# A two-block transformer kernel: a new order of the first loads and turns, and of two short stretches of products

## The reference, cut to what matters

```python
hn = rms_norm(h, norm1_g[i])            # h = x, (256, 1024)
z = hn @ w_in[i]                        # (1024, 3208)
qa, ka, va, qb, kb, vb, ob, ib, fb, uc, vc = split_cols(z, IN_SPLITS)
ya = stick_breaking_attention(qa, ka, va)
qk = jax.nn.silu(causal_depthwise_conv(jnp.concatenate([qb, kb], axis=-1), conv_w[i], conv_b[i]))
hb = mlstm_chunkwise(qb, kb, vb, ib + igate_b[i], fb + fgate_b[i])
...
```

## Time and profile before

| | |
|---|---|
| median of 3 runs | 1088.3 us (1086.83, 1088.3, 1090.26) |
| the profiled execution, its own time | 1087.57 us |
| its span | 1085.6 us |
| PE busy | 1058.6 us, 98% |
| DVE, ACT, POOL busy | 866.3, 714.3, 144.1 us |
| moved from HBM | 230.85 MB, 214 GB/s over the span |

### The profile page before, as it was taken

The page is one execution under the profiler, slowest core; times in us unless marked ns, Lnnn a source line. Parts: engine busy times, 40 slices in busy tenths (PEclk is TensorE's granted clock), DMA queues, the critical chain, the costliest instruction groups (busy, mean ns, idle before and its releaser), DMA issues.

```text
span 1085.6 us, 17366 instructions
## 1 busy us (share of the span) xinstructions
PE 1058.6 (98%) x6390; PEld 925.0 (85%) x6390; DVE 866.3 (80%) x1142; ACT 714.3 (66%) x962; POOL 144.1 (13%) x96
## 2 busy tenths in 40 slices
PE   7999989999999999999999999999999999999997
PEld 6877778888788887789989899998788889999986
DVE  5498689999999999877666777677777877876876
ACT  6676479898889898775435545445566766455553
POOL 3001100000000000012000334250200000432420
PEclk9999999999999999999999999999999999999999
DMA  9541528889988888754654454554433335545531
GB/s 369 189 155 39 206 82 347 348 346 333 346 331 337 343 344 334 285 209 156 225 180 178 155 213 161 206 193 155 173 137 118 116 120 211 207 156 217 184 126 40
DMA packets 33605, 232.64 MB, mean 214 GB/s; under 512 B 3856, under 2 KB 3984, under 8 KB 6032
## 3 DMA queue, kind: packets, MB, share of 16 engines
q1 hardware_dynamic: 32688, 229.98, 57.3%
q10 hardware_dynamic: 864, 1.93, 0.6%
HBM read 230.85 MB, written 1.05 MB: 214 GB/s over the span
## 4 chain that ended last, share of the span: by engine, by line
PE 78%; DVE 12%; ACT 5%; DMA 2%; issue 2%; POOL 0%; SPq 0%; DVEq 0%; ACTq 0%
PE bank L2042 11%; PE bank L2044 11%; PE bank L2043 11%; PE bank L2600 9%; PE bank L2601 8%; PE bank L2602 8%; DVE wlo L1194 4%; PE bank L2449 4%; PE bank L2448 4%; PE bank L2431 2%; ACT whi L529 2%; DMA raw<-stream 2%; DVE arena L1797 2%; PE bank L2456 1%; DVE wlo L1205 1%
## 5 line engine op out<-in xcount | busy, mean ns | idle before, releaser
L1194 DVE TENSOR_TENSOR wlo<-raw,whi 128x2048 fp32r<-128x2048 f32 x178 | 405.7, 2288 | 62.9 <-ACT whi L529 62.3
L529 ACT ACTIVATE whi<-raw 128x2048 fp32r<-128x2048 f32 x197 | 375.0, 1913 | 76.3 <-PE bank L2044 37.6
L2600 PE MATMUL bank<-xs,whi 128*128 128x256 f32 x896 | 251.2, 280 | 1.5 <-DVE wlo L1194 1.5
L2601 PE MATMUL bank<-xs,whi 128*128 128x256 f32 x896 | 250.2, 279 | 0.0
L2602 PE MATMUL bank<-xs,wlo 128*128 128x256 f32 x896 | 250.0, 279 | 0.0
L2600 PEld LDWEIGHTS bank<-xs,whi 128*128 128x128 f32 x896 | 168.4, 188 | 3.8 <-DVE wlo L1194 2.3
L2601 PEld LDWEIGHTS bank<-xs,whi 128*128 128x128 f32 x896 | 168.4, 188 | 0.9
L2602 PEld LDWEIGHTS bank<-xs,wlo 128*128 128x128 f32 x896 | 168.4, 188 | 0.0
L2042 PE MATMUL bank<-whi,rounded 128*128 128x512 f32 x344 | 138.4, 402 | 1.1 <-DVE wlo L1194 0.4
L2044 PE MATMUL bank<-whi,rounded 128*128 128x512 f32 x344 | 136.1, 396 | 0.0
L2043 PE MATMUL bank<-wlo,rounded 128*128 128x512 f32 x344 | 136.0, 395 | 0.0
(11 more groups left out here) (342 smaller groups left out, 1655.2 us busy)
## 6 DMA issues: line engine op xcount, KB each, us to landing
raw<-stream SPq DMA_DIRECT2D x215, 1024.0 KB, 4.9
arena<-finals ACTq DMA_DIRECT2D x3, 512.0 KB, 5.6
xres<-x_in SPq DMA_DIRECT2D x2, 512.0 KB, 4.8
raw<-stream SPq DMA_DIRECT2D x4, 256.0 KB, 6.1
out<-xn SPq DMA_DIRECT2D x4, 256.0 KB, 2.1
par<-params SPq DMA_DIRECT2D x1, 844.0 KB, 12.4
cst<-table SPq DMA_DIRECT2D x1, 502.0 KB, 8.8
arena<-p_in ACTq DMA_DIRECT2D x1, 256.0 KB, 5.9
```

The source lines that it names most:

```text
L529: act.activation(whi[:, s, :], raw[:, a, :], ACT.Copy).then_inc(S("high_done"), 1)
L1194: dve.tensor_tensor(wlo[:, s, :], raw[:, unit0 % RAW, :], whi[:, s, :].bitcast(F32), ALU.subtract)\
L2600: pe.matmul(o, whi[:, s, w], xhi[:, kk, :], start=first, stop=False, skip_group_check=True)
L2601: pe.matmul(o, whi[:, s, w], xlo[:, kk, :], start=False, stop=False, skip_group_check=True)
```

## The change

What it does, in five edits:

1. The identity moves from the table to the head of the parameters, so that identity and gains are one transfer on ACT's queue (96 KB); the table is loaded whole, without it, in its old place.
2. x is loaded by column halves: both tiles' columns 0 to 511, then pieces 0 and 1 of unit 0, both tiles' columns 512 to 1023, then pieces 2 and 3. SP issues eight transfers instead of six ahead of unit 1.
3. PE turns the first half of x (k = 0 to 3, both tiles) at the start and the second half after k = 0 and 1 of the first unit (12 matmuls). ACT and DVE now take: pair 0, piece 0, pair 1, pieces 1, 2, 3, then pairs 2 and 3.
4. k = 0 and 1 of the short chunk (12 matmuls of 136 columns) are issued ahead of `turn_conv_inputs`.
5. k = 2 of chunk 5's second unit (the stream's unit 10; 6 matmuls of 512 columns) is issued ahead of `gate_rows` instead of behind it.

```diff
-CONST, CONST_W = layout([("ident", P), ("later", P), ("ones", P), ("upto", P), ("strict", P), ("bigpast", P),
+CONST, CONST_W = layout([("later", P), ("ones", P), ("upto", P), ("strict", P), ("bigpast", P),
                          ("causal", P), ("cos", TT * HALF), ("sin", TT * HALF), ("iota4", NG), ("iota32", NE),
                          ("neghalf", 8),
                          ("iota64", SLOTS)])
-PARAM, PARAM_W = layout([("g0", KD), ("g1", KD), ("g2", KD), ("g3", KD), ("g4", KD), ("g5", KD), ("g6", KD),
+PARAM, PARAM_W = layout([("ident", P), ("g0", KD), ("g1", KD), ("g2", KD), ("g3", KD), ("g4", KD), ("g5", KD), ("g6", KD),
                          ("g7", KD), ("gates_b", GATES), ("conv_w", 8 * CONV_K), ("conv_b", 8), ("ln_g", SGW),
...
 A_FINAL = 3072
-GAINS = 8 * KD
+GAINS = P + 8 * KD
 A_V = 2048
...
-        ident = C("ident")
+        ident = Q("ident")
         sgu_w = Q("sgu_w").rearrange("p (g t) -> p g t", g=SGG)
...
         def _(sp):
-            for t in range(TT):
-                sp.dma_start(xres[:, t, :], x_in[:, t, :]).then_inc(S(f"x{t}_loaded"), 16)
-            for k in range(4):
-                sp.dma_start(raw[:, 0, cols2(k)], stream[0][:, cols2(k)]).then_inc(S(f"piece{k}_landed"), 16)
+            for c in range(2):
+                for t in range(TT):
+                    sp.dma_start(xres[:, t, cols2(c)], x_in[:, t, cols2(c)]).then_inc(S(f"x_half{c}_loaded"), 16)
+                for k in (2 * c, 2 * c + 1):
+                    sp.dma_start(raw[:, 0, cols2(k)], stream[0][:, cols2(k)]).then_inc(S(f"piece{k}_landed"), 16)
             sp.dma_start(raw[:, 1, :], stream[1]).then_inc(S("landed1"), 16)
-            sp.dma_start(cst[:, P:], table[:, P:]).then_inc(S("table_loaded"), 16)
+            sp.dma_start(cst[:], table).then_inc(S("table_loaded"), 16)
             sp.dma_start(raw[:, 2, :], stream[2]).then_inc(S("landed2"), 16)
...
-            act.dma_start(cst[:, 0:P], table[:, 0:P]).then_inc(S("ident_loaded"), 16)
             act.dma_start(par[:, 0:GAINS], params[:, 0:GAINS]).then_inc(S("gains_loaded"), 16)
             act.wait_ge(S("gains_loaded"), 16)
             act.activation(V("m")[:, 0:1], Q("g0")[:, 0:1], ACT.Copy)
-            for m in range(4):
+            def first_high(m):
                 act.wait_ge(S("turned"), m + 1)
                 for k in (2 * m, 2 * m + 1):
                     ins = act.activation(xhi[:, k, :], turned_k(0, k), ACT.Copy, scale=Q("g0")[:, k:k + 1])
                 ins.then_inc(S("xhi_ready"), 1)
+
+            def piece_high(m):
                 act.wait_ge(S(f"piece{m}_landed"), 16)
                 act.activation(whi[:, 0, cols2(m)], raw[:, 0, cols2(m)], ACT.Copy).then_inc(S("piece_high"), 1)
+
+            first_high(0)
+            piece_high(0)
+            first_high(1)
+            for m in range(1, 4):
+                piece_high(m)
+            first_high(2)
+            first_high(3)
             act.wait_ge(S("landed1"), 16)
...
             dve.wait_ge(S("gains_loaded"), 16)
-            for m in range(4):
+            def first_low(m):
                 dve.wait_ge(S("xhi_ready"), m + 1)
                 for k in (2 * m, 2 * m + 1):
                     dve.scalar_tensor_tensor(xlo[:, k, :], turned_k(0, k), Q("g0")[:, k:k + 1],
                                              xhi[:, k, :].bitcast(F32), ALU.mult, ALU.subtract)\
                        .then_inc(S("xt_ready"), 1)
+
+            def piece_low(m):
                 dve.wait_ge(S("piece_high"), m + 1)
                 dve.tensor_tensor(wlo[:, 0, cols2(m)], raw[:, 0, cols2(m)], whi[:, 0, cols2(m)].bitcast(F32),
                                   ALU.subtract).then_inc(S("piece_low") if m < 3 else S("low_done"), 1)
+
+            first_low(0)
+            piece_low(0)
+            first_low(1)
+            for m in range(1, 4):
+                piece_low(m)
+            first_low(2)
+            first_low(3)
             for c in range(2):
...
+            def turn_first(c):
+
+                pe.wait_ge(S(f"x_half{c}_loaded"), 16 * TT)
+                for k in range(4 * c, 4 * c + 4):
+                    for t in range(TT):
+                        ins = pe.transpose(turned_k(0, k)[:, P * t:P * t + P], xres[:, t, P * k:P * k + P], ident)
+                    if k % 2:
+                        ins.then_inc(S("turned"), 1)
+
             def turn(q):
-
-                for t, ks in ((0, range(4)), (1, range(4)), (0, range(4, KD)), (1, range(4, KD))) if q == 0 else \
-                        [(t, range(KD)) for t in range(TT)]:
-                    if q == 0:
-                        pe.wait_ge(S(f"x{t}_loaded"), 16)
-                    for k in ks:
+                for t in range(TT):
+                    for k in range(KD):
                         if q == 3 and k == 0:
...
-            pe.wait_ge(S("ident_loaded"), 16)
-            turn(0)
+            pe.wait_ge(S("gains_loaded"), 16)
+            turn_first(0)
             def turn_queries():
...
-            def w_in_short():
-                pe.wait_ge(S("act_freed"), SHORT - 1)
-                pe.wait_ge(S("dve_freed"), SHORT - 1)
+            def w_in_short(ks):
+                if ks[0] == 0:
+                    pe.wait_ge(S("act_freed"), SHORT - 1)
+                    pe.wait_ge(S("dve_freed"), SHORT - 1)
                 s = wait_unit(CHUNK_END[SHORT] - 1)
-                for k in range(KD):
+                for k in ks:
                     for t in range(TT):
                         w = slice(TAIL * k, TAIL * k + TAIL)
                         ins = mm3(out_bank(C_WIN + SHORT, t)[:, 0:TAIL], xhi[:, k, P * t:P * t + P],
                                   xlo[:, k, P * t:P * t + P], whi[:, s, w], wlo[:, s, w], start=k == 0, stop=k == 7)
-                ins.then_inc(S("unit_used"), 1)
+                if ks[-1] == KD - 1:
+                    ins.then_inc(S("unit_used"), 1)
...
-            for c in range(2):
-                for u in range(2):
-                    w_in(c, u)
+            w_in(0, 0, (0, 1))
+            turn_first(1)
+            w_in(0, 0, (2, 3))
+            w_in(0, 1)
+            for u in range(2):
+                w_in(1, u)
             w_in(2, 0, (0, 1))
             turn_queries()
             w_in(2, 0, (2, 3))
             for h in range(SBH):
                 scores_a(h)
             w_in(2, 1)
+            w_in_short((0, 1))
             turn_conv_inputs()
-            w_in_short()
+            w_in_short(range(2, KD))
             w_in(4, 0)
             w_in(4, 1)
             w_in(5, 0)
-            w_in(5, 1, (0, 1))
+            w_in(5, 1, (0, 1, 2))
             gate_rows()
-            w_in(5, 1, (2, 3))
+            w_in(5, 1, (3,))
             after(0)
...
     i, j = np.arange(P)[:, None], np.arange(P)[None, :]
-    put("ident", i == j)
     put("later", i > j)
...
+    put("ident", np.eye(P))
     put("g0", cols(norm1_g[0]))
```

## The result

The changed kernel takes 1089.6 us (median of 13 runs, 1087.57 to 1091.79); the kernel before, measured beside it, 1086.74 (13 runs, 1085.79 to 1090.26). The ratio is 1.0023, 95% interval 1.0013 to 1.0034: about 2.5 us slower, within the 0.3% that the prediction called the same. The difference forecast was +2.4 us.

A forecast was written before the change was run, and what follows sets the result against it. PE, busy 98% of the span, was taken as the bound, so edits could only give back its idle time. Profiled 1087.57 + 3.4 (start) - 1.0 (edits 4 and 5) = 1090.0 us, range 1087.0 to 1092.2.

The forecast's parts named there:

- Landing of the half, first product: At the start: half of x lands near 5.1 us, its turn begins about 5.2, first product at 8.9.
- Clock: First products, after PE stands 2 us: 1.2 GHz, 0.45 us each, full clock back 3.5 us after they begin.
- full clock: Rival at the start: clock already up for the first products, +1.7 - 1.0, 1088.3 us; chance 0.25.
- Second turn and the cascade ACT, DVE, unit 2: Turning x's second half costs PE 1.0 us; ACT reaches unit 1 at 15.6, unit 2 is split at 24.3.
- What is late next is unit 2: Start: PE would be free before unit 2 is split, and takes it at 24.4, 3.4 us later.
- near 23.7: Start: when PE's products of unit 1's second half end, before unit 2 is split at 24.3 us.
- Start, in all: Edits at the start: PE takes unit 2 at 24.4 instead of 21.03 us, 3.4 us later.
- Late edits: Edits 4 and 5, up to the gate rows: 1.0 us gained by both together, bounds 0 and 1.4.
- 0.4 later: Turn of the convolution's inputs: 1.35 us of matmuls in a 0.9 us stand begin it at about 49.1, not 48.70.
- Unit 2 is in time: Rival at the start: PE alone counts and reaches chunk 1 at the same 21.1, 1086.6 us; chance 0.08.
- Late clock: Rival at the start: clock returns only after the second turn, +4.8 - 1.0, 1091.4 us; chance 0.14.
- The sum: Whole kernel: profiled execution 1087.57 + 3.4 for the start - 1.0 for edits 4 and 5 = 1090.0 us.

The follow-up runs named there:

- x4: Changed kernel with the four squares of the norm moved behind ACT's part of unit 2: 1089.46 us, ratio 1.0022 to the kernel before.
- x3: Changed kernel with nine more transposes, whose output nobody reads, right behind the first turn: 1088.24 us, ratio 1.0011 to the kernel before.
- x8: Kernel before with edits 4 and 5, and 20 matmuls on a constant tile ahead of the first turn: 1087.51 us, ratio 1.0013.
- x9: Kernel before with edits 4 and 5, and 10 matmuls on a constant tile ahead of the first turn: 1085.83 us, ratio 0.9996.
- x6: Kernel before with edit 5 alone: 1085.68 us, ratio 0.9989.
- x7: Changed kernel with nine unread transposes behind the first turn and the norm's squares behind unit 2: 1088.51 us, ratio 1.0017 to the kernel before.
- x2: Changed kernel with edits 4 and 5 undone, only the start new: 1091.07 us, ratio 1.0036 to the kernel before.
- x1: Kernel before with edits 4 and 5 alone: 1085.83 us against 1087.07, ratio 0.9992.
- x10: Kernel before with edits 4 and 5 alone, the same kernel as x1 measured again: 1084.66 us against 1086.0, ratio 0.9987.
- x5: Kernel before with edit 4 alone: 1086.27 us against 1086.3, ratio 1.0001.

## Why the prediction was right

- **Landing of the half, first product.** 5.25 and 8.95 us, forecast 5.2 and 8.9. Rows of 2 KB cost x nothing that can be seen; the slow stretch came while the pieces were under way (225 GB/s from 5 to 6 us): ACT waited 0.65 us each for two of them, and PE had products to issue meanwhile.
- **Clock.** The level and its cost were right: the first eight products at half rate, the return after 3.5 us of work (in x4 it took 4.4), and by x3 1.4 us at the 49th product. The row it was taken from supports it less than it seems. At 146 us the clock was up before the stand; at the start it had not come up, and where it had, a stand of 1.5 us did not bring it down (x8, x9). Behind the same stand at 148 to 150 us (2.35 us) after's next three matmuls took 0.93 us instead of 1.52, and the clock fell only at 152.4. So the forecast was right that the first products would be slow; that the stand is the cause isn't shown, and choosing by one row was in part luck. That "the waits of 0.9 us elsewhere never show a lower clock", under "full clock", holds for before; in x3 and x6 the clock fell in such a wait, at 110.6 and 110.4 us. The Trainium skill (TensorE: Matmul & The Clock Gate, Part 1), by which the lower level is the default and activity lifts it, agrees with x3. Its Part 4, by which transposes don't bring the full clock, doesn't: the row of L2141 in x3 falls to 345 ns on average, and the products behind it run at the high level from the first; in x7 the same transposes stay at 421.
- **Second turn and the cascade ACT, DVE, unit 2.** 15.5 us for unit 1 on ACT, forecast 15.6. "What is late next is unit 2" was right, and so was PE's own end, 23.67 against "near 23.7". But it means that unit 2 decides over the last 0.5 us only: the second turn, the slow products and the wait for unit 1 lie in PE's own path, and x4 took unit 2 out of the way with nothing gained in the median, where 0.5 us would hardly be seen.
- **Start, in all.** 3.1 us in the trace, 3.9 in the medians of x2 (2.4 to 5.4), forecast 3.4.
- **Late edits.** 1.4 us between the traces of before and x1, 1.2 between those of x2 and after, 1.3 in the medians (x10, 0.4 to 2.3), forecast 1.0. The term that was mis-sized is the delay of the turn, "0.4 later": it was 0.25, because the hole was 1.05 us and not 0.9. The mechanism, DVE's delay carried to the gate rows, holds between x2 and after. Between before and x1 it doesn't, since before's trace has 0.25 us more at line 634; why is open. The wait at the gate rows, forecast to be still 0.4, is 0.2.
- **Rivals.** "Full clock" is what x3 built by hand: +1.2 us by the median, +0.7 forecast, and +1.7 at the 49th product in both. "Unit 2 is in time" was tried in x4 and x7: it is not enough. "Late clock" did not come in any profile; x4's 0.8 us later return is a step towards it. (Its 1091.4 us are 0.35% above the base, not 0.34%.)
- **The sum** 1090.0 lies 0.4 above the median, from a base (1087.57) that stood 0.8 above the median measured later. The difference, +2.4 against +2.5 by the ratio, is closer than its terms, which is luck: 3.4 - 1.0 stands where the medians have 3.9 - 1.3 and the traces of before and after 3.1 - 1.3. Which of these two is nearer can't be told; the intervals of the medians hold both.

## What to carry to other kernels

At the start of a kernel, a transfer that lands earlier gives PE a head start only if PE can stay busy from there: here 0.8 us of head start bought a stand of 1.8 us, products at the lower clock for 3.5 us, and transposes in the path that had been hidden behind a wait. In before the slow stretch of the start fell on the transposes, where it cost little. Ask of moved PE work who waits for its output: the other two engines' whole queue stood behind the second turn. And a gap filled ahead of a chain that doesn't need PE is only worth something if work is also moved ahead of that chain's end, as x5 shows against x1.

## What the runs showed of the hardware

The clock also fell where PE never stood. In x5 it is half from 91 us on, right behind eight matmuls with four rows of partitions, and PE was busy all the time (windows of x5, PE alone: length, busy, granted clock, DMA share, GB/s):

```profile
88.00:91.00 3.00, 3.00 (x12) 0.95 0.00 0
91.00:94.00 3.00, 3.00 (x10) 0.50 0.00 0
```

In x4 it fell at the same place, at about 91.8 us, behind the same eight matmuls. In before and after it did not fall there, though the same matmuls ran; it fell once in each near 150 us. In x3 and x6 it fell near 110 us, in a stand of 0.9 us that before and after have there too, and in x6 it stayed at half until 117 us. In x5 the first product of w_out came at 119.45 us for it, 1.5 later than in before. Besides, PE's waits for ACT in the experts' stage differ with the same instructions. Over the whole span, first before, then after:

```profile
PE bank L2456 <- ACT arena L754: 2.3, 6, 0.7
```

```profile
PE bank L2487 <- ACT arena L764: 0.8, 2, 0.5
```

Each of these two is 1.5 us between a pair of traces, and together they are as large as the difference looked for. Of the 1.8 us by which after is late at w_out's first product, its shorter waits in the experts take back 1.5, so that the spans differ by only 0.6 where the medians differ by 2.9. That these waits vary by chance, and not because of the change, isn't shown by this pair; x2, with the same start, has 2.2 us of them. For such reasons each cause was read at a fixed instruction (the 49th product, the gate rows, the first product of w_out) and its worth in the intervals. What makes the clock fall in one execution and not in the next, and what makes the waits in the experts differ, was not tried.
